# Two of the four weight sums of a seven-product matrix application made by accumulating transfers from HBM

## The reference

```
def swiglu(u, w_gate, w_up, w_down):
    return (jax.nn.silu(u @ w_gate) * (u @ w_up)) @ w_down
```

## Time and profile before

| | |
|---|---|
| time, median of 3 runs | 2842.44 us (2842.32 to 2842.53) |
| span of the profiled execution | 2833.9 us |
| TensorE busy | 2813.9 us, 99% |
| VectorE busy | 2029.3 us, 72% |
| ScalarE busy | 1471.8 us, 52% |
| GpSimd busy | 25.2 us, 1% |
| HBM read | 511.63 MB, 181 GB/s over the span |

### The profile page before, as it was taken

One profiled execution on the slowest core, in us unless ns is written; L12 is line 12 of the kernel. 1 busy time (PEld: TensorE's weight loads), 2 busy tenths in 40 slices (PEclk: granted clock), 3 DMA queues, 4 the chain that ended last, 5 costly groups with the idle time before them and its releaser, 6 DMA issues.

```text
span 2833.9 us, 38622 instructions
## 1 busy us (share of the span) xinstructions
PE 2813.9 (99%) x14909; PEld 2332.1 (82%) x14909; DVE 2029.3 (72%) x2719; ACT 1471.8 (52%) x1915; POOL 25.2 (1%) x43
## 2 busy tenths in 40 slices
PE   9999999999999999999999999999999999999998
PEld 8888888888888888888888888888888887888887
DVE  5786865688878887564545588888888667876555
ACT  5554465655545554455455465555555546455444
POOL 0000000000000000000000000000000100000000
PEclk9999999999999999999999999999999999999999
DMA  7543346565655656555554556656665754444553
GB/s 246 178 149 120 120 149 208 178 207 201 220 203 196 216 200 231 194 189 183 168 174 151 191 186 207 215 194 207 207 205 201 251 190 146 149 155 164 197 178 134
DMA packets 256219, 528.28 MB, mean 186 GB/s; under 512 B 9536, under 2 KB 10016, under 8 KB 255056
## 3 DMA queue, kind: packets, MB, share of 16 engines
q1 hardware_dynamic: 250096, 501.61, 52.4%
q0 software_dynamic: 2816, 13.20, 1.4%
q10 hardware_dynamic: 3168, 11.54, 1.0%
HBM read 511.63 MB, written 2.10 MB: 181 GB/s over the span
## 4 chain that ended last, share of the span: by engine, by line
PE 97%; DVE 1%; ACT 1%; issue 0%; DMA 0%; DVEq 0%; ACTq 0%
PE acc L645 67%; PE acc L696 12%; PE side L1113 2%; PE side L1116 2%; PE side L1112 2%; PE acc L1112 1%; PE acc L1116 1%; PE acc L1113 1%; PE side L965 1%; PE acc L752 1%; PE side L798 1%; PE side L958 1%; PE side L850 1%; PE side L1104 0%; ACT ar L1557 0%
## 5 line engine op out<-in xcount | busy, mean ns | idle before, releaser
L2418 DVE TENSOR_TENSOR wlo<-raw,whi 128x1024 fp32r<-128x1024 f32 x532 | 644.8, 1223 | 444.2 <-ACT whi L1568 442.4
L1568 ACT ACTIVATE whi<-raw 128x1024 fp32r<-128x1024 f32 x532 | 557.0, 1059 | 486.3 <-PE acc L645 473.0
L645 PE MATMUL acc<-whi,xh 128*128 128x512 f32 x2152 | 593.2, 397 | 0.2 <-issue 0.2
L1971 ACT ACTIVATE whi<-raw 128x1024 fp32r<-128x1024 f32 x360 | 379.9, 1061 | 402.1 <-PE acc L696 142.0
L645 PE MATMUL acc<-wlo,xh 128*128 128x512 f32 x2152 | 576.8, 390 | 0.2
L645 PE MATMUL acc<-whi,xl 128*128 128x512 f32 x2152 | 576.3, 390 | 0.0
L2928 DVE TENSOR_TENSOR wlo<-raw,whi 128x1024 fp32r<-128x1024 f32 x360 | 438.1, 1222 | 100.9 <-ACT whi L1971 93.0
L645 PEld LDWEIGHTS acc<-wlo,xh 128*128 128x128 f32 x2152 | 403.4, 188 | 86.9 <-DVE wlo L2418 2.2
L645 PEld LDWEIGHTS acc<-whi,xl 128*128 128x128 f32 x2152 | 404.0, 188 | 86.2
L645 PEld LDWEIGHTS acc<-whi,xh 128*128 128x128 f32 x2152 | 394.2, 188 | 78.1 <-issue 0.6
L645 PE MATMUL acc<-whi,hTh 128*128 128x512 f32 x672 | 182.0, 393 | 0.0
(11 more groups left out here) (395 smaller groups left out, 2848.1 us busy)
## 6 DMA issues: line engine op xcount, KB each, us to landing
raw<-in_ffn_w_down SPq DMA_DIRECT2D x88, 1024.0 KB, 5.0
raw<-in_ffn_w_gate SPq DMA_DIRECT2D x68, 1024.0 KB, 5.0
raw<-in_ffn_w_up SPq DMA_DIRECT2D x68, 1024.0 KB, 5.0
raw<-in_ev_w_in SPq DMA_DIRECT2D x56, 1024.0 KB, 5.0
raw<-in_od_w_in SPq DMA_DIRECT2D x48, 1024.0 KB, 5.0
raw<-in_w_in SPq DMA_DIRECT2D x32, 1024.0 KB, 5.2
raw<-in_ffn_w_gate SPq DMA_DIRECT2D x40, 512.0 KB, 3.7
raw<-in_ffn_w_up SPq DMA_DIRECT2D x40, 512.0 KB, 4.5
```

Of the source, the lines that this page charges most:

```text
L645: mm = pe.matmul(acc[2 * pair + t][:], x[:, k0 + j, t * P:t * P + P], w[:, ring, j], start=start and j == 0, stop=stop and j == 1)
L1568: act.activation(whi[:, place % RING], raw_granule(place), ACT.Copy).then_inc(S("hi_done"), 1)
L1971: act.activation(o, src, ACT.Copy).then_inc(S("hi_done"), 1)
L2418: dve.tensor_tensor(wlo[:, place % RING], raw_granule(place), whi[:, place % RING].bitcast(F32), ALU.subtract).then_inc(S("lo_done"), 1)
```

## The change

In every mixed pair two of the four sums are no longer made by VectorE. GpSimd issues a transfer that adds gate row tile k from HBM onto b1 in place (`raw_added`). For wx, SP loads up row tile k into wx (`wx_part`, `wx_in`) and GpSimd issues a transfer that adds up row tile k+1 (`wx_added`). `sums_two` stays on VectorE. SP loads wx for pair one behind its wait for slot 0 of the block, and for pair two when VectorE has made the low part of granule 5 out of wx, between slots 5 and 6. ScalarE waits for these transfers where it waited for VectorE's first two sums. Counts of semaphores are changed to match (in the recurrence of the first mixer, three semaphores are folded into others, and two for late loads into one).

```diff
+
+ADDED0, _a = {}, 0
+for _n, _nc, _ in LINEARS:
+    if _n[:2] == "up":
+        ADDED0[_n] = _a
+        _a += _nc // 2 - (1 if _n[3] == "a" else 0)
+
+
+def added(name, i, parts=1, n=0):
+
+    return i * 16 * parts + 16 * (parts * (ADDED0[name] - (1 if name[3] == "a" else 0)) + n + 1)
+
+
+def raw_count(name, i, m):
+
+    n = SLOT0[name] + 8 + m
+    step = LANDED[n + 8] - LANDED[n]
+    return i * step + (LANDED[n] - step)
 
 
...
+
+                    def wx_part(k, cl):
+                        sp.dma_start(wx, w[:, k, cl]).then_inc(S("wx_in"), 16)
+
                     for m in range(8):
                         if name[3] == "a":
                             slot(n0 + m, (g if m < 4 else w)[:, 4 * (m % 4):4 * (m % 4) + 4, cl])
@@ -371,9 +394,22 @@
                         else:
                             k0 = 2 * m if m < 5 else 4 * (m - 5)
                             slot(n0 + m, (g if m < 5 else w)[:, k0:k0 + 4, cl])
+                        if name[3] == "b" and m == 1:
+                            sp.wait_ge(S("lo_done"), FREE[n0 + 1 - RING] + 1)
+                            wx_part(12, cl)
+                        if name[3] == "b" and m == 5:
+                            sp.wait_ge(S("lo_done"), block_start(name) + 6)
+                            wx_part(14, cl)
+                    if name[3] == "a":
+                        sp.wait_ge(S("xmix_done"), XMIX0[name] + 10)
                     with sp.Fori(1, nch // 2) as i:
                         cl = bass.ds(first * CH + i * CH, CH)
                         for m in range(8):
+                            if m == 1:
+                                wx_part(12, cl)
+                            if m == 6:
+                                sp.wait_ge(S("lo_done"), i * MIXED + (block_start(name) + 6))
+                                wx_part(14, cl)
                             sp.wait_ge(S("lo_done"), i * MIXED + (FREE[n0 + 12 + m] - 2 * MIXED))
...
+            def sums_block(name, i):
+
+                l = int(name[2])
+                g, w = kview(A["ffn_w_gate"][l]), kview(A["ffn_w_up"][l])
+                first = 0 if name[3] == "a" else FF_A
+                cl = slice(first * CH, first * CH + CH) if isinstance(i, int) else bass.ds(first * CH + i * CH, CH)
+
+                def here():
+
+                    pool.wait_ge(S("x_in2"), 16)
+
+                def raw_sum(m, k):
+                    pool.wait_ge(S(f"landed{m}"), raw_count(name, i, m))
+                    here()
+                    pool.dma_start(raw[:, m, 1], g[:, k, cl], accum_op=ALU.add).then_inc(S(f"raw_added{m}"), 16)
+
+                def wx_sum(k, second):
+                    pool.wait_ge(S("wx_in"), added(name, i, 2, second))
+                    here()
+                    pool.dma_start(wx, w[:, k, cl], accum_op=ALU.add).then_inc(S("wx_added"), 16)
+
+                wx_sum(13, 0)
+                raw_sum(1, 12)
+                raw_sum(3, 14)
+                wx_sum(15, 1)
+
+            def sums(name):
+                with pool.Fori(1, CHUNKS[name] // 2) as i:
+                    sums_block(name, i)
+
             pool.wait_ge(S("xl_done"), 2 * 8 * TOF["up0a"])
             pool.dma_start(h[:], A["x"][0].rearrange("(t p) n -> p t n", p=P)).then_inc(S("gdn_rows_in"), 16)
+            sums("up0a")
+            sums_block("up0b", 0)
             pool.wait_ge(S("used"), GRAN0["up0b"])
             pool.dma_start(pc[:, 0:768], A["c_odd"]).then_inc(S("masks_in"), 16)
+            sums("up0b")
             gain_row(1, A["ffn_norm_post"][0], "used", GRAN0["dn0b"])
             gain_row(2, A["mix_norm_post"][1], "ug_done", 16)
+            sums("up1a")
+            sums_block("up1b", 0)
+            sums("up1b")
             gain_row(3, A["ffn_norm_post"][1], "used", GRAN0["dn1b"])
...
-                pe.wait_ge(S("r_done"), 6 * hg + 1)
+                pe.wait_ge(S("r_done"), 7 * hg + 1)
                 pe.wait_ge(S("inv_step0"), 30 * hg + 30)
                 b = claim(side[0], "vn_done", 2 * hg + 1)
                 mm4(b, lambda k: U0(MT_)[:, k], lambda k: U0(LM_)[:, k]).then_inc(S("vn_ready"), 1)
                 beside()
                 pe.wait_ge(S("vn_done"), 2 * hg + 1)
-                pe.wait_ge(S("kd_done"), hg + 1)
+                pe.wait_ge(S("r_done"), 7 * hg + 3)
                 b = claim(side[1], "s_done", hg + 1)
...
                     def sums(n):
-                        act.wait_ge(S("wmix_done"), i * 8 + (wmix_start(name) + n - 8))
+                        act.wait_ge(S("wmix_done"), i * 4 + (wmix_start(name) + n - 4))
 
                     def clean(idx, m, n):
                         if n == 0:
@@ -1983,12 +2055,13 @@
                         hi(idx, raw[:, m % RING, 2 * n:2 * n + 2])
 
                     def mixed(idx, m, n):
-                        full(m)
+                        act.wait_ge(S(f"landed{m}"), raw_count(name, i, m))
                         hi(idx, raw[:, m, 0::2])
+                        act.wait_ge(S(f"raw_added{m}"), added(name, i))
+                        hi(idx + 1, raw[:, m, 1::2])
                         sums(n + 2)
-                        hi(idx + 1, raw[:, m, 1::2])
-                        sums(n + 4)
                         hi(idx + 2, raw[:, m, 0::2])
+                        act.wait_ge(S("wx_added"), added(name, i, 2, int(n > 0)))
                         hi(idx + 3, wx)
 
...
-                    mixed(8, 3, 4)
+                    mixed(8, 3, 2)
...
-                    def sums_one(idx, m, n):
-                        dve.wait_ge(S("hi_done"), i * MIXED + (v0 + idx + 1))
-                        dve.wait_ge(S("lo_done"), i * MIXED + (v0 + idx))
-                        b = raw[:, m]
-                        tt(wx, b[:, 1], b[:, 3], ALU.add, "wmix_done")
-                        dve.wait_ge(S("wmix_done"), i * 8 + (wmix_start(name) + n + 1 - 8))
-                        tt(b[:, 1], b[:, 0], b[:, 1], ALU.add, "wmix_done")
-
                     def sums_two(idx, m, n):
                         dve.wait_ge(S("lo_done"), i * MIXED + (v0 + idx + 1))
                         b = raw[:, m]
-                        dve.wait_ge(S("wmix_done"), i * 8 + (wmix_start(name) + n + 2 - 8))
+                        dve.wait_ge(S(f"raw_added{m}"), added(name, i))
                         tt(b[:, 0], b[:, 1], b[:, 3], ALU.add, "wmix_done")
-                        dve.wait_ge(S("wmix_done"), i * 8 + (wmix_start(name) + n + 3 - 8))
+                        dve.wait_ge(S("wmix_done"), i * 4 + (wmix_start(name) + n + 1 - 4))
                         tt(b[:, 2], b[:, 0], b[:, 2], ALU.add, "wmix_done")
 
...
-                    sums_one(2, 1, 0)
                     lo(2, raw[:, 1, 0::2])
...
-                    sums_one(8, 3, 4)
                     lo(8, raw[:, 3, 0::2])
-                    sums_two(8, 3, 4)
+                    sums_two(8, 3, 2)
                     lo(9, raw[:, 3, 1::2])
```

More of the change, by code:

```diff
@@ L66 @@
         if _n[3] == "a":
-            _w, _m, _h, _x = _w + 4 * _nc - 8, _m + 4 * _nc - 6, _h + _nc // 2 + 1, _x + 14
+            _w, _m, _h, _x = _w + 2 * _nc - 4, _m + 4 * _nc - 6, _h + _nc // 2 + 1, _x + 14
         else:
-            _w, _m, _h = _w + 4 * _nc, _m + 4 * _nc, _h + _nc // 2
+            _w, _m, _h = _w + 2 * _nc, _m + 4 * _nc, _h + _nc // 2
     if _n in ("dn0a", "dn1a"):
@@ L152, in wmix_start @@
 def wmix_start(name):
-    return WMIX0[name] + (0 if name[3] == "a" else 8)
+    return WMIX0[name] + (0 if name[3] == "a" else 4)
+ADDED0, _a = {}, 0
[9 more added lines that the diff above has]
+    return i * step + (LANDED[n] - step)
 def round_of(name, i):
@@ L524, in _ @@
             pool.dma_start(at(WPOOL, 8, 256), A["w_pool_2"][0].rearrange("g (k p) d -> p (g k) d", p=P))\
-                .then_inc(S("wpool_in"), 16)
+                .then_inc(S("late_in"), 16)
             pool.wait_ge(S("pool_mixed"), 4)
@@ L529, in _ @@
             pool.dma_start(at(PIN, TT, 256), A["p_2"][0, 0].rearrange("(t p) n -> p t n", p=P))\
-                .then_inc(S("p_in"), 16)
+                .then_inc(S("late_in"), 16)
         dtb, alog, onorm = grow[:, 0:8], grow[:, 8:16], grow[:, 128:256]
@@ L1059, in _ @@
                 pe.wait_ge(S("s_done"), hg + 1)
-                b = claim(side[3], "r_done", 6 * hg + 6)
-                mm4(b, lambda k: U1(KT)[:, k], lambda k: U0(KT)[:, k]).then_inc(S("ks_ready"), 1)
+                b = claim(side[3], "r_done", 7 * hg + 7)
+                mm4(b, lambda k: U1(KT)[:, k], lambda k: U0(KT)[:, k]).then_inc(S("s_ready"), 1)
                 b = claim(side[1], "qs_done", 4 * (hg + 1))
-                mm4(b, lambda k: U1(QT)[:, k], lambda k: U0(KT)[:, k]).then_inc(S("qs_ready"), 1)
+                mm4(b, lambda k: U1(QT)[:, k], lambda k: U0(KT)[:, k]).then_inc(S("s_ready"), 1)
                 beside()
-                pe.wait_ge(S("r_done"), 6 * hg + 6)
+                pe.wait_ge(S("r_done"), 7 * hg + 7)
                 b = claim(side[0], "vn_done", 2 * hg + 2)
```

(14 more changed lines are left out.)

## The result

The changed kernel is slower by 0.14%: 2842.22 us median of 20 runs against 2838.19 us of 20 runs of the kernel before, ratio 1.0014, interval 1.0008 to 1.0021, so about 4 us. The number 2842.4 that was forecast is met by chance only. The three runs shown before were all of one kind: this kernel's times stand in groups near 2835.7, 2838.2 and 2842.4 us, with a granted TensorE clock over the span of 0.999, 0.998 to 0.999, and 0.996 in the runs that list it. The whole range moved: the lowest time is 2838.97 against 2835.47 us, the highest 2847.03 against 2842.79. What was forecast was no effect, and there is one.

A forecast was written before the change was run, and what follows sets the result against it. TensorE was taken as the bound, with no idle time in a mixed block of 42.87 us. 0 removed plus 0 added left 2842.4 us (span 2833.9 us), range 2841.0 to 2872.

The forecast's parts named there:

- rival 1: Pair two's accumulating wx transfer exceeds 6.15 us, delaying TensorE's last product: 2859 us at 7.0, 2889 at 8.5; chance 0.25.
- The likeliest case: Pair two's wx sum lands at 1777.2, 0.8 us inside the limit, so no effect; chance 0.66.
- VectorE's relief is worth 0: Mixed blocks: removing 80 additions, 55 us of VectorE time, gains 0, because TensorE stays at 42.87 us a block.
- The relief moves what hangs on it by 0.93 us: Pair one: the hidden product and all behind it start 0.93 us earlier; slot 5's load goes out at 1765.9, not 1766.77.
- The limit: Pair two: the wx sum must land by 1778.0 for TensorE's last product, allowing the accumulating transfer 6.15 us.
- The load of wx lands 5.65 us after slot 5's issue: Pair two: 5.0 us for slot 5's 1 MB ahead, plus 0.65 for the load's own 256 KB.
- the allowance of 0.3 us: Pair two: estimated time for GpSimd to wake and work out the dynamic address after the wx load lands.
- The accumulating transfer takes 5.35 us: Pair two's wx sum, issue to landing: 4.7 us for 256 KB plus 0.65 for reading the target.
- Traffic is free: Weight loads in mixed blocks absorb 1.5 MB more per block within 8 us of slack; rival of delayed loads, chance 0.02.
- GpSimd is not locked out: GpSimd's issues don't wait for VectorE; the rival of one VectorE instruction's wait, 1.22 us, gave 2851 us, chance 0.04.

The follow-up runs named there:

- short_sums: Also experiment 3: kernel before, the two sums per mixed pair that the change removes shortened to 8 of 512 columns, no transfers added; ratio 0.9998.
- experiment 4: Changed kernel, SP's load of slot 6 held back in the 18 looped blocks until pair two's wx sum has landed; ratio 0.9997.
- experiment 5: Changed kernel, slot 5's load, with the wx load behind it, held back by one more low part (0.7 us) in looped blocks; ratio 1.0006.
- experiment 2: Changed kernel, one pair's sums back on VectorE: transfers for pair one only, ratio 0.9995; transfers for pair two only, ratio 1.0004.
- experiment 6: Changed kernel, two single runs: pair two's wx load behind slot 6, 2935.4 us; pair two's second wx transfer plain instead of accumulating, 2836.2 us.

## Why the prediction was wrong

The place of the loss, its order of waits and its slope were named under rival 1. The condition that rival 1 gives did not come true: the accumulating transfer stayed under 6.15 us, but it started 1.1 us later than the prediction had it. The likeliest case, that the chain ends 0.8 us inside the limit, was wrong by that much. Point by point:

- *VectorE's relief is worth 0:* right (short_sums; 42.87 us of TensorE in the earlier trace rows). There is nothing to be gained in these blocks by taking work from VectorE.
- *The relief moves what hangs on it by 0.93 us:* nearly. Slot 5 goes out 6.71 us after TensorE's start on the block, 7.44 before, so 0.73 earlier; I had 6.57.
- *The limit:* right. The prediction's 1778.0 is 18.67 us after the block's start at 1759.33. In the changed kernel no block lost time where ScalarE started on wx 18.53 us after the start or earlier, and each did from 18.71 on; at 18.94, in the block shown, TensorE lost 0.28.
- *The load of wx lands 5.65 us after slot 5's issue:* **the step that failed.** It was built from landing times of the kernel before, where slot 5 follows hm_turn by 1.7 us. Measured, the load of wx goes out 0.60 us behind slot 5 and lands 5.6 us later (median of the 18 looped blocks): 6.2. The 0.65 us that I gave to its 256 KB was right; slot 5 in front of it was late. In the block shown, GpSimd issues the sum 6.89 us after slot 5, where 5.65 + 0.3 = 5.95 was taken. Moving slot 5 forward by 0.7 us, which I counted as a gain, put it closer to hm_turn's 512 KB, which I had not named at all; slot 5 lands in 5.5 us, 5.0 in the earlier trace rows. The wake-up is part of it: from the landing of the load to GpSimd's issue it is 0.62 us in nearly every block, so the allowance of 0.3 us was short by some 0.3 too. Experiments 3, 4 and 5 part the two disturbances: hm_turn's is 0.3 to 0.4 us on the loads, slot 6's 1.0 us on the sum. About 0.1 us more is there at the old distance from hm_turn too (experiment 2: 5.2 against 5.0); its cause was not tested.
- *The accumulating transfer takes 5.35 us:* 5.34 from issue to ScalarE in the block shown; pair two's land in 5.2 us in the median. The number came out right by luck, its reason was wrong: without slot 6 it is 4.2, and the rest was the 1 MB of slot 6 on the same engines (experiment 4). I had that overlap among the arguments for rival 1 and gave it no number.
- *Traffic is free:* right for the weight loads themselves. ScalarE waited for a slot (raw, gate) in three blocks, 3.1 us at most in the trace, without TensorE.
- *GpSimd is not locked out:* right. Of its 80 issues 78 took 0.83 to 0.90 us and two 1.19, with VectorE busy for 78% of the mixed blocks (424.18 us of the 547.00 from 557 to 1104). The Trainium skill's warning (SBUF — State Buffer, Summary: rules for kernel authors) did not show here. The page gives it for VectorE in its 2x and 4x modes, and the prediction took it to hold for any VectorE instruction. What mattered is another statement of the Trainium skill, in Trainium Kernel Development and Optimization, Key Constraints, that the queues of SP, ACT and POOL all run on the same 16 DMA engines and interleave there. Here the trace agrees: 5.2 us for pair two's transfer beside slot 6, 4.2 without it.

In the block shown the chain is late against the prediction by 0.14 (slot 5's issue) + 0.94 (from there to GpSimd's issue) - 0.01 (the transfer) = 1.07 us. The margin was 0.8, which leaves 0.27, and TensorE lost 0.28. Over the 20 blocks the loss is 3.7 us. The chance of 0.25 for that rival was too low for a margin of 0.8 us on a sum of four terms, none of them priced beside the transfers that it would meet. That the median of 2842.22 us lies next to the forecast of 2842.4 is luck, as said above.

## What to carry to other kernels

Where the busiest engine has no gap, taking work from another can only lose; the question is then which new chain has the least slack. A chain of two dependent transfers and a wake-up must be priced with the transfers that will be on the engines at that time, also those of other queues: the medians of the kernel before were too short here by 0.4 us. Relief of an engine also moves the transfers that wait for it, and can move them next to others. If such a chain is short of slack, the order of issue on the queue (the small load that something waits for, ahead of the large one that has 8 us of slack) repairs it for nothing: here it brings the changed kernel level with the one before, and no version is shown to be faster than that one, since TensorE is full.

## What the runs showed of the hardware

- An accumulating transfer of 256 KB from HBM into SBUF takes the engines about 1.0 us more than a plain one (good to 0.3 us) and 144 packets against 80. It lands in 4.2 us (4.0 at least) where no 1 MB load is beside it or one was issued 3.1 us ahead, and in 5.2 us where one was issued 2.8 us ahead (medians of pair two's).
- A 512 KB copy within SBUF and a 1 MB load from HBM issued 1.0 us apart were both slower by 0.3 to 0.4 us than 1.6 to 1.7 us apart (hm_turn 3.2 to 3.3 against 2.9 us, slot 5 5.5 against 5.0 to 5.2).
- From the landing of a load to GpSimd's issue of the transfer that waits for it, 0.62 us pass where GpSimd works out the address in a loop, and 0.28 us in the two blocks outside the loops. The issue itself takes 0.84 us for an accumulating transfer in both places, and 0.57 for the plain one in its stead (experiment 6).
- The granted clock fell to 0.50 (1.2 GHz) for 6.83 us, beginning within a run of 128 small matmuls, at the same two places of the traces of the changed kernel and of experiments 3 and 4, and at neither in the trace of the kernel before. The two falls together cost about 6.2 us, more than the effect that was studied. It also fell for 3.41 us or more behind 17 of 20 waits of TensorE of 3.1 to 4.0 us (experiment 6), and behind none of the waits of 0.4 us.
